# Head means of three projections: one float32 matmul becomes two rounded matmuls, of the rounded square and of its rest

## What is computed

```python
def l2norm(x):                                     # gated delta rule (GDN): q and k, 4 heads of 128
    return x * lax.rsqrt(jnp.sum(x * x, axis=-1, keepdims=True) + 1e-6)

def rms_norm(x, gain=None):                        # second block: q and k of each head of 64
    xf = x.astype(F32)
    y = xf * lax.rsqrt(jnp.mean(xf * xf, axis=-1, keepdims=True) + EPS)
    ...
```

## Time and profile before

| what | before |
|---|---|
| three runs, us | 2448.03, 2449.57, 2449.85; median 2449.57 |
| profiled execution, span from the first to the last instruction, us | 2447.7 |
| PE / DVE / ACT / POOL busy | 98% / 61% / 39% / 34% |
| chain that ended last, by engine | PE 84%, DVE 7%, issue 4%, ACT 3%, POOL 2% |
| GDN projection in the trace | about 133 to 231 us |
| differential projection | about 786 to 885 us |
| neighborhood projection | about 970 to 1082 us |

### The profile page before, as it was taken

The page is one execution under the profiler, slowest core; times in us unless marked ns, Lnnn a source line. Parts: engine busy times, 40 slices in busy tenths (PEclk is TensorE's granted clock), DMA queues, the critical chain, the costliest instruction groups (busy, mean ns, idle before and its releaser), DMA issues.

```text
span 2447.7 us, 37094 instructions
## 1 busy us (share of the span) xinstructions
PE 2394.9 (98%) x14385; PEld 1959.5 (80%) x14385; DVE 1495.8 (61%) x2056; ACT 958.7 (39%) x1531; POOL 831.6 (34%) x454
## 2 busy tenths in 40 slices
PE   8999999999999999999999999999999999999999
PEld 6778877888886878866888888888887758788887
DVE  5765755547666976585466766644778586524242
ACT  4566644232224645356342222122266332423232
POOL 2533033544442222233223323223234313354443
PEclk9999999999999999999999999999999999999999
DMA  7212023445441110120224434323311111232322
GB/s 251 87 63 84 3 69 119 138 147 180 138 142 39 61 35 20 52 76 2 69 95 137 147 120 138 113 94 95 129 65 47 61 60 61 86 112 95 101 97 86
DMA packets 64662, 227.41 MB, mean 93 GB/s; under 512 B 7040, under 2 KB 9088, under 8 KB 63882
## 3 DMA queue, kind: packets, MB, share of 16 engines
q1 hardware_dynamic: 51160, 176.05, 21.5%
q10 hardware_dynamic: 13362, 49.40, 6.1%
HBM read 223.30 MB, written 2.12 MB: 92 GB/s over the span
## 4 chain that ended last, share of the span: by engine, by line
PE 84%; DVE 7%; issue 4%; ACT 3%; POOL 2%; DMA 0%; SPq 0%; DVEq 0%; POOLq 0%; ACTq 0%
PE ps L277 23%; PE ps L278 23%; PE ps L279 23%; PE ps L1064 2%; PE ps L1324 2%; POOL w_lo L3401 1%; PE ps L1286 1%; DVE rstd L963 1%; PE ps L1081 1%; PE ps L1094 1%; PE ps L1304 1%; PE ps L362 1%; PE ps L361 1%; PE ps L360 1%; PE ps L3173 1%
## 5 line engine op out<-in xcount | busy, mean ns | idle before, releaser
L3401 POOL TENSOR_TENSOR w_lo<-ring,w_hi 128x1024 fp32r<-128x1024 f32 x288 | 703.9, 2444 | 1167.2 <-ACT w_hi L270 664.6
L277 PE MATMUL ps<-act_hi,w_hi 128*128 128x512 f32 (+1 forms) x2280 | 844.0, 370 | 8.5 <-DVE act_lo_mixer L605 2.9
L279 PE MATMUL ps<-act_hi,w_lo 128*128 128x512 f32 (+1 forms) x2280 | 829.7, 364 | 0.0
L278 PE MATMUL ps<-act_lo_ffn,w_hi 128*128 128x512 f32 (+1 forms) x1408 | 513.6, 365 | 0.0
L277 PEld LDWEIGHTS ps<-act_hi,w_hi 128*128 128x128 f32 x2280 | 430.0, 189 | 95.3 <-issue 13.8
L279 PEld LDWEIGHTS ps<-act_hi,w_lo 128*128 128x128 f32 x2280 | 429.3, 188 | 72.0
L270 ACT CAST w_hi<-ring 128x1024 fp32r<-128x1024 f32 (+1 forms) x167 | 172.7, 1034 | 627.1 <-PE ps L279 569.3
L1715 ACT CAST w_hi<-ring 128x1024 fp32r<-128x1024 f32 (+1 forms) x132 | 137.5, 1044 | 456.9 <-PE ps L279 456.9
L278 PEld LDWEIGHTS ps<-act_lo_ffn,w_hi 128*128 128x128 f32 x1408 | 265.6, 189 | 41.0
L1604 DVE SCALAR_TENSOR_TENSOR ada_place<-ada_place 128x1024 f32<-128x1024 f32 x180 | 279.8, 1554 | 24.5 <-DMA ada_place<-in_w_ada 10.1
L277 PE MATMUL ps<-hidden_hi,w_hi 128*128 128x512 f32 (+1 forms) x704 | 256.5, 364 | 1.8 <-DVE hidden_lo L1801 1.5
(11 more groups left out here) (465 smaller groups left out, 3224.7 us busy)
## 6 DMA issues: line engine op xcount, KB each, us to landing
ring<-in_w_ffn SPq DMA_DIRECT2D x204, 512.0 KB, 3.3
ada_place<-in_w_ada ACTq DMA_DIRECT2D x90, 512.0 KB, 4.2
ring<-in_w_gdn SPq DMA_DIRECT2D x16, 512.0 KB, 3.3
ring<-in_w_hy SPq DMA_DIRECT2D x12, 512.0 KB, 3.3
ring<-in_w_dil_qk SPq DMA_DIRECT2D x8, 512.0 KB, 8.7
ring<-in_w_out SPq DMA_DIRECT2D x8, 512.0 KB, 3.2
ring<-in_w_diff_qk SPq DMA_DIRECT2D x8, 512.0 KB, 3.3
ring<-in_w_na_qk SPq DMA_DIRECT2D x8, 512.0 KB, 3.3
```

The lines of the kernel that those rows point to most:

```text
L277: pe.matmul(out, w[0], x[0], start=start, stop=False)
L278: pe.matmul(out, w[0], x[1], start=False, stop=False)
L279: return pe.matmul(out, w[1], x[0], start=False, stop=stop)
L3401: pool.tensor_tensor(k.w_lo[:, a % SPLITS, :], k.ring[:, a % SLOTS, :], k.w_hi[:, a % SPLITS, :].bitcast(F32), ALU.subtract).then_inc(k.lo ...
```

## The change

The square in `sq` gets a rounded part `squares_hi`, a cast on ScalarE which first waits for the square's own completion (`link`), and a rest `squares_lo`, a subtraction on GpSimd. The rest is written in place over `sq`; the rounded part has a place of its own. TensorE then adds up two rounded matmuls, of the two parts, with rounded copies of the constant matrices (`means`), which three casts on ScalarE make once, at the start of the GDN projection. The root, the reciprocal and the multiply stay. GpSimd's program for the stages is written out, with the subtractions between the rests of the weights.

```diff
@@ Projection.tensor
-                last = pe.matmul(k.bank(6), mean, k.sq[:, j % 2, 0:S], start=True, stop=True)
-                if size > S:
-                    last = pe.matmul(k.bank(7, size - S), mean, k.sq[:, j % 2, S:size], start=True, stop=True)
+                for out, a, b in ((k.bank(6), 0, S), (k.bank(7, size - S), S, size)):
+                    pe.matmul(out, mean, k.squares_hi[:, j % 2, a:b], start=True, stop=False)
+                    last = pe.matmul(out, mean, k.squares_lo[:, j % 2, a:b], start=False, stop=True)
@@ Projection.scalar, square(i)
-            s.eng.activation(k.sq[:, i % 2, 0:size], src, ACT.Square).then_inc(self.squares, 1)
+            link(s, s.eng.activation(k.sq[:, i % 2, 0:size], src, ACT.Square))
+            s.eng.copy(k.squares_hi[:, i % 2, 0:size], k.sq[:, i % 2, 0:size]).then_inc(k.sem("head_squares_hi"), 1)
@@ Projection, new
+    def gpsimd(self, pool, lower_unit):
+        k, n, u0 = self.k, self.tiles, FIRST[self.name]
+
+        def lower_square(i):
+            if i >= len(self.jobs):
+                return
+            size = self.jobs[i][0].shape[-1]
+            pool.wait_ge(k.sem("head_squares_hi"), self.b + i + 1)
+            pool.tensor_tensor(k.squares_lo[:, i % 2, 0:size], k.sq[:, i % 2, 0:size], k.squares_hi[:, i % 2, 0:size].bitcast(F32),
+                               ALU.subtract).then_inc(self.squares, 1)
+
+        for i, events in enumerate(self.slots):
+            if i < n + self.units - 1:
+                lower_unit(u0 + i + SPLITS)
+            if i <= n:
+                lower_square(i)
+            for j in events:
+                if j >= n - 1:
+                    lower_square(j + 2)
+        lower_unit(u0 + n + self.units - 1 + SPLITS)
@@ gdn_project_tensor
-            pe.matmul(k.bank(5 + 2 * (j % 2)), k.const("ones"), k.sq[:, j % 2, 0:S], start=True, stop=True)\
-                .then_inc(k.sem("head_summed"), 1)
+            out = k.bank(5 + 2 * (j % 2))
+            pe.matmul(out, k.means[:, 2, :], k.squares_hi[:, j % 2, 0:S], start=True, stop=False)
+            pe.matmul(out, k.means[:, 2, :], k.squares_lo[:, j % 2, 0:S], start=False, stop=True).then_inc(k.sem("head_summed"), 1)
@@ gdn_project_scalar, silu(j)
-            s.eng.activation(k.sq[:, j % 2, 0:S], x[:, j, :], ACT.Square).then_inc(k.sem("head_squares"), 1)
+            link(s, s.eng.activation(k.sq[:, j % 2, 0:S], x[:, j, :], ACT.Square))
+            s.eng.copy(k.squares_hi[:, j % 2, 0:S], k.sq[:, j % 2, 0:S]).then_inc(k.sem("head_squares_hi"), 1)
@@ gpsimd_program
+            for j in range(16):
+                lower(FIRST["w_gdn"] + j + SPLITS)
+                if 1 <= j <= 8:
+                    pool.wait_ge(k.sem("head_squares_hi"), j)
+                    pool.tensor_tensor(k.squares_lo[:, (j - 1) % 2, 0:S], k.sq[:, (j - 1) % 2, 0:S],
+                                       k.squares_hi[:, (j - 1) % 2, 0:S].bitcast(F32), ALU.subtract).then_inc(k.sem("head_squares"), 1)
@@ scalar_program
     act.wait_ge(k.loaded_late, 48)
+    for i, name in enumerate(("heads64", "heads128", "ones")):
+        act.copy(k.means[:, i, :], k.const(name))
     gdn_project_scalar(k, s)
```

More of the change, by code:

```diff
@@ L177, in __init__ @@
         self.pair_turned = self.over(ada_at + 4 * 2 * T, "pair_turned", 4 * T)
+        self.squares_hi = self.over(ada_at + 4 * 4 * T, "squares_hi", 2 * T, R32).rearrange("p (s n) -> p s n", s=2)
+        self.squares_lo = self.over(ada_at, "squares_lo", 2 * T, R32).rearrange("p (s n) -> p s n", s=2)
         self.consts = self.place("consts", NCONST)
@@ L181, in __init__ @@
         self.small = self.place("small", 128)
+        self.means = self.place("means", 3 * P, R32).rearrange("p (s n) -> p s n", s=3)
         self.ps = ctx.enter_context(nc.psum_tensor("ps", [P, 8 * 512], F32))
@@ L2044, in na_project @@
     return Projection(k, "w_na_qk", 8, "w_na_v", 4, HALF, val, 16, 8, 8, jobs=
-                      [(q[:, t, :], k.const("heads64"), k.par("na_q_down"), "eps_query", float(HD), None) for t in range(4)]
-                      + [(key[:, t, :], k.const("heads64"), k.par("na_k"), "eps", 1.0, None) for t in range(4)]
-                      + [(k.mix[:, t, :], k.const("heads128"), k.par("subln"), "eps_subln", SUBLN, None)
+                      [(q[:, t, :], k.means[:, 0, :], k.par("na_q_down"), "eps_query", float(HD), None) for t in range(4)]
+                      + [(key[:, t, :], k.means[:, 0, :], k.par("na_k"), "eps", 1.0, None) for t in range(4)]
+                      + [(k.mix[:, t, :], k.means[:, 1, :], k.par("subln"), "eps_subln", SUBLN, None)
                          for t in range(4)])
@@ L2053, in diff_project @@
     return Projection(k, "w_diff_qk", 8, "w_diff_v", 4, HALF, val, 8, 0, 0, jobs=
-                      [(q[:, t, :], k.const("heads64"), k.par("da_q"), "eps_query", float(HD), k.par("da_q_swap")) for t in range(4)]
-                      + [(key[:, t, :], k.const("heads64"), k.par("da_k"), "eps", 1.0, k.par("da_k_swap")) for t in range(4)])
+                      [(q[:, t, :], k.means[:, 0, :], k.par("da_q"), "eps_query", float(HD), k.par("da_q_swap")) for t in range(4)]
+                      + [(key[:, t, :], k.means[:, 0, :], k.par("da_k"), "eps", 1.0, k.par("da_k_swap")) for t in range(4)])
 GQA = 28
@@ L3434, in gpsimd_program @@
         if stage == "diff":
-            lower_units(done, FIRST["w_ffn1"] + SPLITS)
+            lower_units(done, FIRST["w_gdn"] + SPLITS)
+            for j in range(16):
[4 more added lines that the diff above has]
+                                       k.squares_hi[:, (j - 1) % 2, 0:S].bitcast(F32), ALU.subtract).then_inc(k.sem("head_squares"), 1)
+            lower_units(FIRST["w_gdn"] + 16 + SPLITS, FIRST["w_ffn1"] + SPLITS)
             added_beside(k, pool, k.view(k.big, 0, DT, S), 0)
@@ L3439, in gpsimd_program @@
             done = FIRST["w_diff_qk"] + SPLITS
-        lower_units(done, FIRST[values] + units + SPLITS)
+        if stage in ("diff", "na"):
+            project = (diff_project if stage == "diff" else na_project)(k)
+            project.gpsimd(pool, lambda u: lower_units(u, u + 1))
+        else:
+            lower_units(done, FIRST[values] + units + SPLITS)
         done = FIRST[values] + units + SPLITS
```

## The result

| | before | after |
|---|---|---|
| median of the runs, us | 2449.57 (13 runs, 2448.03 to 2449.95) | 2454.17 (13 runs, 2452.21 to 2456.51) |
| ratio | | 1.002, 95% interval 1.0013 to 1.0027 |
| span of the profiled execution, us | 2447.7 | 2454.5 |
| mean granted clock of TensorE | 0.997 | 0.994 |

A forecast was written before the change was run, and what follows sets the result against it. TensorE, busy 98% of the span, was taken to bound the kernel, with ScalarE and VectorE within 5% in the GDN stage. Terms +4.1 - 1.9 - 2.8 = -0.6 us gave 2449.0 us, range 2443.5 to 2455.0.

The forecast's parts named there:

- The sum: Whole kernel: the three stage terms added, +4.1 - 1.9 - 2.8 = -0.6 us, giving 2449.0 us.
- GDN: GDN projection: ScalarE's added cast sets the round, last sum 4.5 us later, less 0.39 for its shortening: +4.1 us.
- differential: Differential projection: first sum uncovered, +2.8 us; later ones covered, eight shortened sums give back 4.7: -1.9 us.
- neighborhood: Neighborhood projection: seven covered sums give -4.1 us, VectorE's last multiply ends about 1.3 later: -2.8 us.
- Part 1, the sums: TensorE, all three stages: 0.86 us becomes 0.47 and 1.29 becomes 0.70, 14.9 us gross over 28 sums.
- Parts 2 and 3, the cast and the subtraction: After each square: ScalarE cast of 0.63 or 0.82 us, then GpSimd subtraction of 1.35 or about 1.85 us.
- The first differential sum: Start of the differential stage: cast and subtraction stand uncovered before the sum, delaying it 2.8 us.
- The neighborhood tail: Sum of tile 8 starts 2.6 us later behind GpSimd's weight rest; VectorE's last multiply ends about 1.3 later.
- both claims on the lock: Neighborhood, VectorE against GpSimd's shared port: one multiply freed, giving 2.1 us back; another newly caught, about +1.5 us.
- B: Rival: partly free ScalarE slots in the GDN stage take the cast; total -5.8 us, 2443.8 us; chance 0.16.
- C: Rival: VectorE's GDN multiplies wait on GpSimd's doubled work through the port lock; 6 us more, 2455.0 us; chance 0.18.
- the sign: GDN stage: long two-input multiplies on VectorE with ScalarE idle would speak for C.

The follow-up runs named there:

- warm_waits3: The full change, plus 15, 12 and 18 matmuls that change nothing, filling TensorE's three long waits; 2449.1 us, ratio 1.0 against the kernel before.
- plain_two: Kernel before with the change in differential and neighborhood stages only, except the first differential sum and that of neighborhood tile 8; 2439.92 us, ratio 0.9965.
- gdn_alone3: Kernel before with the change in the GDN stage alone, the other two stages as before; 2455.28 us, ratio 1.0028.
- full_again: The full change measured once more, beside other kernels on the same chip; 2454.4 us, ratio 1.002 against the kernel before.
- gdn_one_rounded: Kernel before with GDN sums of the rounded square alone, no cast or subtraction, other stages as before; 2446.97 us, ratio 0.9993.

## Why the prediction was wrong

**The step that failed** is "The sum": "+4.1 - 1.9 - 2.8 = -0.6 us". Every wait in it was priced by its length, and three waits of 3.2 to 4.7 us on TensorE were each followed by a stretch at 1.2 GHz, which cost 6.6 us in the profiled execution. No term and no rival had that. By place, in the profiled execution of after:

| place | forecast | half clock | rest | measured |
|---|---|---|---|---|
| GDN | +4.1 | +2.85 | +0.3 | +7.3 |
| differential | -1.9 | +1.55 | +0.7 | +0.4 |
| neighborhood | -2.8 | +2.24 | -0.3 | -0.9 |
| sum | -0.6 | +6.6 | +0.7 | +6.8 |

The rest is what the two columns before it leave over; 0.6 of it is a wait in the differential stage (below). The measured column is how far the rows of TensorE, in the last stage those of VectorE, fell back over the stage. GDN: TensorE began to wait for the first sum at 149.66 before and 149.89 after; the last sum is at 197.05 and 204.95; 7.90 - 0.23 - 0.39 for its shortening. Differential: from 785.99 and 793.67 (the last unit ahead, +7.68) to 884.68 and 892.74 (the attention's first products, +8.06). Neighborhood: from the first sums at 979.43 and 987.19 (+7.76) to VectorE's last multiply at 1081.34 and 1088.21 (+6.87). What little is left lies between the stages, and the spans differ by 6.8. The half clock elsewhere cancels: its windows outside the three stages cost both profiled executions about 7 us (5 us windows, each length times one minus its granted clock, added up). The medians differ by only 4.6: the execution profiled is the longest of after, and the stretches vary from one execution to the next (below).

**Right, step by step.**
- *Part 1, the sums*: two rounded matmuls start 0.23 us apart, and later differential rounds are 9.09 long (812.22 to 821.31); 9.1 was forecast.
- *Parts 2 and 3, the cast and the subtraction*, and ScalarE as the engine that sets the GDN round from the third sum on. ScalarE's timeline of after, one slot of the GDN stage, answers to the earlier trace rows:

```profile
169.65 1.04 ACT L273 CAST w_hi<-ring 128x1024 fp32r<-128x1024 f32 x1
...
173.26 0.63 ACT L2539 ACTIVATE sq<-big 128x512 f32<-128x512 f32 x1
173.93 0.62 ACT L2540 CAST squares_hi<-sq 128x512 fp32r<-128x512 f32 x1
174.57 1.28 ACT L2547 ACT_TABLE_LOAD   x1
...
176.45 1.04 ACT L273 CAST w_hi<-ring 128x1024 fp32r<-128x1024 f32 x1
```

  Gapless, 6.80 us from split to split; 6.76 was forecast. The subtraction that follows the cast ending at 174.55 on GpSimd took 1.28 (1.35 forecast), and 768 columns took 1.84 (1.85) where nothing held it up.
- *GDN without the clock*: in warm_waits3 the sums take 48.40 us from first to last, before 45.59; with 2.0 for the first wait and 0.39 back that is +4.4, against +4.1. So the delays were added up rightly, and the +7.3 of after is not a mis-sized cast. The same holds for the other two stages at full clock. From the first differential sum to the first neighborhood sum warm_waits3 takes 184.17 us and before 188.40, so -4.2, and with the +2.8 of the first sum -1.5, against -1.9. From there to VectorE's last multiply it takes 98.88, before 101.91: -3.0, against -2.8. The three make -0.1 us, and its ratio is 1.0.
- *The first differential sum*: +2.8 forecast, +2.76 measured (10.44 later, in a stage entered 7.68 later). One slack was thinner than said: the first value unit now waits 0.61 us for ScalarE's copy.
- *The neighborhood tail*: the sum of tile 8 stands 5.54 us behind that of tile 7 (1050.61 to 1056.15), before 2.97: +2.57, where 2.6 was forecast. On VectorE both claims on the lock hold, the multiply that is freed and the one that is newly caught; engines here hold each other up without a semaphore too. VectorE's timeline of after, answering to the earlier trace rows, and GpSimd's row it met:

```profile
1065.43 1.02 DVE L990 SCALAR_TENSOR_TENSOR mix<-mix,params,rstd 128x768 f32<-128x768 f32 x1
1069.59 4.95 DVE L988 RECIPROCAL rstd<-probs 128x768 f32<-128x768 f32 x1 [3.14 <-ACT probs L944]
...
1080.62 2.57 DVE L990 SCALAR_TENSOR_TENSOR mix<-mix,params,rstd 128x768 f32<-128x768 f32 x1
...
1088.21 1.02 DVE L990 SCALAR_TENSOR_TENSOR mix<-mix,params,rstd 128x768 f32<-128x768 f32 x1
```

```profile
1079.97 2.40 POOL L3428 TENSOR_TENSOR w_lo<-ring,w_hi 128x1024 fp32r<-128x1024 f32 x1 [6.96 <-ACT w_hi L273]
```

  The multiply took 1.55 us more than 1.02 and ended 0.8 behind GpSimd's (+1.5 forecast). The same 2.57 stands in warm_waits3, at full clock. But the reciprocal at 1069.59 waited 3.14 us for its root, where the one in warm_waits3 waited 0.99: TensorE came late out of the half clock.

**The rivals.** B (the saving comes through) fell: GDN rounds are 6.79, not 6.1. C (the lock in the GDN stage) fell too, although the sign was its own: VectorE's eight multiplies there take 691 to 695 ns in after, as before (0.69), and TensorE's waits in the stage are for GpSimd's rest of the square behind a full ScalarE.

## What to carry to other kernels

Price a new wait on a busy TensorE by its length and by what the granted clock does behind it: here waits of 3.2 to 4.7 us cost another 1.4 to 2.9 us each, in every trace that has them bare. Split a shortening by its places: where a step with added latency has other work ahead of it, take it; where it stands bare, keep the old form (plain_two gains 9.5 us by leaving 10 of 28 sums as they were). And before shortening work on the leading engine, look who is second: in the GDN stage VectorE and ScalarE stood within 5%.

## What the hardware showed that was not expected

- The same wait does not cost the same each time. Behind the identical 3.79 us wait the first GDN round took 9.34 (after), 8.07 (gdn_alone3) and 7.90 us (full_again). Behind the wait of 2.4 us later in the stage after had none and full_again a stretch of 0.8 us. The 13 runs of after have spans of 2450.2 to 2450.9, 2452.0 to 2452.7 and 2454.5 us with mean granted clocks of 0.996, 0.994 to 0.995 and 0.994: the longer the span, the lower the clock. The Trainium skill ("TensorE: Matmul & The Clock Gate", Part 1) says the gate passes one of two levels and that the number of slow matmuls varies from run to run of one kernel; the traces agree.
- Length alone doesn't say whether the clock falls. The 1.80 us wait before the first GDN sum left it at 1.00 in the kernel before, but in gdn_one_rounded, with a wait of the same 1.80 us, 150 to 165 us shows 0.89. The longest wait of all, 6.8 us for the input at the start of before, is followed by 1.00 from 5 to 25 us. What decides it was not tested.
- The kernel before has such stretches too, at places that the change doesn't touch. Behind a wait of 1.73 us at 1783 us its clock is 0.74 (1785 to 1790); after shows 1.00 there behind the same wait. Behind a wait of 2.36 us at 2017 us before shows 1.00, and after 0.85 and 0.80 (2020 to 2030).
- Part of the scatter has nothing to do with the change: in the first 50 us the profiled executions of before and after both show a clock of 0.97, those of the experiments 1.00. The experiments' rows therefore stand some 2 us earlier, and between them and before or after only distances are compared above.
